# A decoder trunk on one core: four row additions placed inside VectorE's last expert round, and the closing norm worked tile by tile on three engines

## The reference

```python
logits = (x @ w_router).astype(jnp.float32) + b_router.astype(jnp.float32)
top_vals, top_idx = lax.top_k(logits, TOP_K)            # TOP_K = 2 of 8
weights = jax.nn.softmax(top_vals, axis=-1)
gates = jnp.sum(jax.nn.one_hot(top_idx, N_EXPERTS) * weights[..., None], axis=-2)
for e in range(N_EXPERTS):
    out = out + gates[..., e:e + 1] * swiglu(x, w_gate[e], w_up[e], w_down[e])
...
h = h + moe_ffn(...)
return rms_norm(h, final_norm)                          # mean of squares, rsqrt, times a gain
```

## Time and profile before

| | |
|---|---|
| time, median of 3 runs | 1004.39 us (1003.5 to 1005.32) |
| profiled execution, first to last instruction | 1002.2 us |
| PE busy | 981.9 us, 98% |
| DVE busy | 757.2 us, 76% |
| ACT busy | 656.1 us, 65% |
| POOL busy | 63.2 us, 6% |
| granted TensorE clock, mean | 0.996 of full speed |

### The profile page before, as it was taken

The page is one execution under the profiler, slowest core; times in us unless marked ns, Lnnn a source line. Parts: engine busy times, 40 slices in busy tenths (PEclk is TensorE's granted clock), DMA queues, the critical chain, the costliest instruction groups (busy, mean ns, idle before and its releaser), DMA issues.

```text
span 1002.2 us, 14574 instructions
## 1 busy us (share of the span) xinstructions
PE 981.9 (98%) x4892; PEld 830.1 (83%) x4892; DVE 757.2 (76%) x915; ACT 656.1 (65%) x886; POOL 63.2 (6%) x86
## 2 busy tenths in 40 slices
PE   8999999999999999999999999999999999999995
PEld 7988887888888899988887888888888888888883
DVE  4657665456456566766688989898998989899888
ACT  5555345453445445554697887978879787887964
POOL 1301000000000100000070000000000000000141
PEclk9999999999999999999999999999999999999998
DMA  9743589994666657243669999999999999999992
GB/s 321 231 165 126 189 249 304 289 327 154 205 203 207 210 163 201 93 136 105 221 233 398 398 383 409 390 401 378 390 375 384 406 371 400 377 382 392 381 404 108
DMA packets 150537, 287.12 MB, mean 286 GB/s; under 512 B 12770, under 2 KB 58866, under 8 KB 150499
## 3 DMA queue, kind: packets, MB, share of 16 engines
q1 hardware_dynamic: 147890, 277.64, 78.3%
q0 software_dynamic: 2608, 8.98, 2.6%
HBM read 269.81 MB, written 16.78 MB: 286 GB/s over the span
## 4 chain that ended last, share of the span: by engine, by line
PE 82%; DVE 8%; ACT 4%; DMA 3%; issue 2%; POOL 1%; SPq 0%; ACTq 0%; DVEq 0%; POOLq 0%
PE A L584 21%; PE A L586 21%; PE A L585 21%; PE S L584 4%; PE S L586 4%; PE S L585 4%; DVE lo L1608 3%; PE T L629 3%; ACT hi L1158 2%; DMA raw<-in_moe_w_down 1%; PE T L1093 1%; DMA raw<-in_moe_w_up 1%; PE T L664 1%; PE T L1051 1%; PE S L675 1%
## 5 line engine op out<-in xcount | busy, mean ns | idle before, releaser
L1608 DVE TENSOR_TENSOR lo<-raw,hi 128x1024 fp32r<-128x1024 f32 (+4 forms) x532 | 571.2, 1130 | 121.4 <-ACT hi L1158 119.4
L1158 ACT ACTIVATE hi<-raw 128x1024 fp32r<-128x1024 f32 (+4 forms) x532 | 485.5, 981 | 146.9 <-PE A L586 120.9
L584 PE MATMUL A<-lo,xT_hi 128*128 128x512 f32 x820 | 324.0, 395 | 1.7 <-DVE lo L1608 1.6
L586 PE MATMUL A<-hi,xT_hi 128*128 128x512 f32 x820 | 319.9, 390 | 0.0
L585 PE MATMUL A<-hi,xT_lo 128*128 128x512 f32 x820 | 319.6, 390 | 0.0
L584 PEld LDWEIGHTS A<-lo,xT_hi 128*128 128x128 f32 x820 | 154.2, 188 | 34.1 <-DVE lo L1608 2.4
L586 PEld LDWEIGHTS A<-hi,xT_hi 128*128 128x128 f32 x820 | 154.0, 188 | 32.4
L585 PEld LDWEIGHTS A<-hi,xT_lo 128*128 128x128 f32 x820 | 154.2, 188 | 30.3
L584 PE MATMUL S<-lo,xT_hi 128*128 128x512 f32 x224 | 89.1, 398 | 0.7 <-DVE lo L1608 0.5
L586 PE MATMUL S<-hi,xT_hi 128*128 128x512 f32 x224 | 87.5, 391 | 0.0
L585 PE MATMUL S<-hi,xT_lo 128*128 128x512 f32 x224 | 87.4, 390 | 0.0
(11 more groups left out here) (239 smaller groups left out, 871.2 us busy)
## 6 DMA issues: line engine op xcount, KB each, us to landing
raw<-in_moe_w_down SPq DMA_DIRECT2D x64, 896.0 KB, 9.2
raw<-in_moe_w_gate SPq DMA_DIRECT2D x32, 768.0 KB, 7.8
raw<-in_moe_w_up SPq DMA_DIRECT2D x24, 768.0 KB, 7.0
raw<-in_moe_w_gate SPq DMA_DIRECT2D x16, 1024.0 KB, 6.7
raw<-in_moe_w_up SPq DMA_DIRECT2D x32, 512.0 KB, 6.6
raw<-in_moe_w_up SPq DMA_DIRECT2D x16, 1024.0 KB, 7.8
raw<-in_ff_w_gate SPq DMA_DIRECT2D x10, 1024.0 KB, 8.4
raw<-in_ff_w_up SPq DMA_DIRECT2D x10, 1024.0 KB, 7.7
```

What stands on the lines that cost most here:

```text
L584: nc.tensor.matmul(out, stat[0], mov[1], start=start, stop=False)
L586: return nc.tensor.matmul(out, stat[0], mov[0], start=False, stop=stop)
L1158: return nc.scalar.activation(out, in_, ACT.Copy)
L1608: nc.vector.tensor_tensor(piece(lo, SPLIT, u, i), piece(raw, RAW, u, i), piece(hi, SPLIT, u, i).bitcast(F32), ALU.subtract).then_inc(lo_do ...
```

## The change

Five edits, all in the last round and behind it.

1. DVE's loop runs one round less (`final` = rounds - 1, computed and loaded as `nfinal`), and the body of the last round is written out behind it. In it the four `add_rows` stand behind the split of U+9: one ahead of `hidden_lo(1)`, three between it and the splits of U+10 and U+11.
2. Behind the last split come `output_lo(0)`, `output_lo(1)` and the four `add_output` in the order (0,0), (1,0), (0,1), (1,1). ACT's squares take the same order.
3. The adding of the two sums goes from POOL to DVE (`mean`); POOL is left with the power.
4. Of tile 1 DVE multiplies both halves by the gain ahead of the norm's factor; the first half then takes one multiplication on DVE (L2234 of the changed kernel), the second one on ACT as before. ACT starts the transfer of its quarter itself; SP starts three.
5. On POOL the product that gives `row_from` goes ahead, and the one that gives `gate_row` takes its place behind the wait for the stored rows.

The diff, cut to its changed lines:

```diff
@@ -329,6 +329,7 @@
         nround = sb("nround", [P, 1], I32)
+        nfinal = sb("nfinal", [P, 1], I32)
         slot_of = sb("slot_of", [P, NT, E])
@@ -388,7 +389,7 @@
         gates_set = sem("gates_set")
-        last_gained, last_out = sem("last_gained"), sem("last_out")
+        last_gained, mean_set, final_set = sem("last_gained"), sem("mean_set"), sem("final_set")
         xs_hi, xs_done = sem("xs_hi"), sem("xs_done")
@@ -432,7 +433,7 @@
 
-        gained, out_last = R2[:, 0:512], R2[:, 512:D]
+        gained, out_last = R2[:, 0:D], R2[:, D:D + 512]
         junk, junk_v, junk_end = R3[:, 3072:4096], R3[:, 2048:3072], R1[:, D:2 * D]
@@ -537,14 +538,10 @@
                     expert_loads(e, e + E)
-            for n, (t, c) in enumerate(((0, 0), (0, 1), (1, 1), (1, 0))):
+            for t, c in ((0, 0), (0, 1), (1, 0)):
                 cols = slice(c * 512, (c + 1) * 512)
-                if n == 2:
-                    sp.wait_ge(last_out, 1)
-                else:
-                    sp.wait_ge(xn_done, XN_OF["final"] + 2 * t + c + 1)
-                sp.dma_start(out[0, t * P:(t + 1) * P, cols], out_last if n == 2 else xn[:, t, cols]
-                             ).then_inc(out_done, 16)
+                sp.wait_ge(xn_done, XN_OF["final"] + 2 * t + c + 1)
+                sp.dma_start(out[0, t * P:(t + 1) * P, cols], xn[:, t, cols]).then_inc(out_done, 16)
             sp.wait_ge(out_done, 16 * 2 * NT)
@@ -1579,7 +1576,7 @@
             for n in range(4):
-                t, c = divmod(n, 2)
+                c, t = divmod(n, 2)
                 cols = slice(c * 512, (c + 1) * 512)
@@ -1588,7 +1585,9 @@
             act.wait_ge(rstd_done, N_FINAL + NT)
-            nc.scalar.activation(out_last, gained, ACT.Copy, scale=scaled(N_FINAL, 1)).then_inc(last_out, 1)
+            nc.scalar.activation(out_last, gained[:, 512:D], ACT.Copy, scale=scaled(N_FINAL, 1)).then_inc(act_step, 1)
+            act.wait_ge(act_step, 1)
+            act.dma_start(out[0, P:2 * P, 512:D], out_last).then_inc(out_done, 16)
 
@@ -2094,6 +2093,7 @@
             nc.vector.tensor_tensor(r1[:, 2, :], top[:, :, 1], top[:, :, 0], ALU.subtract).then_inc(ahead_set, 1)
+            nc.vector.tensor_scalar(nfinal[:, :], r1[:, 7, 1:2], float(E - 1), None, ALU.add).then_inc(final_set, 1)
             split(U_MOE, 0, (2,))
@@ -2159,9 +2159,11 @@
             dve.wait_ge(route_done, 1)
+            dve.wait_ge(final_set, 1)
             rounds = dve.value_load(nround[0:1, 0:1], min_val=E, max_val=2 * E)
+            final = dve.value_load(nfinal[0:1, 0:1], min_val=E - 1, max_val=2 * E - 1)
             U, t1 = U_MOE, T_MOE + 2
-            with dve.Fori(0, rounds) as ve:
+            def first_units(ve):
                 split(U + 2, ve)
@@ -2175,35 +2177,62 @@
                 split(U + 9, ve)
+
+            with dve.Fori(0, final) as ve:
+                first_units(ve)
                 hidden_lo(1, t1 + 2, ve)
...
                 split(U + 11, ve)
-                with dve.If(ve < rounds - 1):
-                    gathered_lo(t1 + 4, ve)
-                    split(U, ve + 1)
-                    split(U + 1, ve + 1)
+                gathered_lo(t1 + 4, ve)
+                split(U, ve + 1)
+                split(U + 1, ve + 1)
+
+            first_units(final)
             dve.wait_ge(gates_set, 1)
             dve.wait_ge(y_back, 16 * 2 * NT)
-            for k in range(2):
-                add_rows(k, 0)
+            add_rows(0, 0)
+            hidden_lo(1, t1 + 2, final)
+            add_rows(1, 0)
+            add_rows(0, 1)
+            add_rows(1, 1)
+            split(U + 10, final)
+            split(U + 11, final)
             output_lo(0)
-            add_rows(0, 1)
             output_lo(1)
-            add_output(0, 0)
-            add_output(0, 1)
-            add_rows(1, 1)
-            add_output(1, 0)
-            add_output(1, 1)
+            for c in range(2):
+                for t in range(NT):
+                    add_output(t, c)
             dve.wait_ge(gb2_in, 48)
+
+            def gained_last(c):
+
+                cols = slice(c * 512, (c + 1) * 512)
+                ins = nc.vector.tensor_tensor(gained[:, cols], h[:, 1, cols], GB2[:, cols], ALU.mult)
+                if c:
+                    ins.then_inc(last_gained, 1)
+                else:
+                    step(ins)
+
+            def mean(t):
+
+                dve.wait_ge(tile_summed, NT + t + 1)
+                nc.vector.tensor_scalar(rstd[:, N_FINAL, t:t + 1], half_sum[:, t, 0:1], half_sum[:, t, 1:2], EPS,
+                                        ALU.add, ALU.add).then_inc(mean_set, 1)
+
             dve.wait_ge(rows_added, 4)
-            nc.vector.tensor_tensor(gained, h[:, 1, 512:D], GB2[:, 512:D], ALU.mult).then_inc(last_gained, 1)
+            gained_last(1)
+            mean(0)
+            gained_last(0)
+            mean(1)
             dve.wait_ge(xrow_in, rounds * 16)
-            for t in range(NT):
-                dve.wait_ge(rstd_done, N_FINAL + t + 1)
-                for c in range(2 - t):
-                    cols = slice(c * 512, (c + 1) * 512)
-                    nc.vector.scalar_tensor_tensor(xn[:, t, cols], h[:, t, cols], rstd[:, N_FINAL, t:t + 1],
-                                                   GB2[:, cols], ALU.mult, ALU.mult).then_inc(xn_done, 1)
+            dve.wait_ge(rstd_done, N_FINAL + 1)
+            for c in range(2):
+                cols = slice(c * 512, (c + 1) * 512)
+                nc.vector.scalar_tensor_tensor(xn[:, 0, cols], h[:, 0, cols], rstd[:, N_FINAL, 0:1],
+                                               GB2[:, cols], ALU.mult, ALU.mult).then_inc(xn_done, 1)
+            dve.wait_ge(rstd_done, N_FINAL + 2)
+            nc.vector.tensor_scalar(xn[:, 1, 0:512], gained[:, 0:512], rstd[:, N_FINAL, 1:2], None, ALU.mult
+                                    ).then_inc(xn_done, 1)
 
@@ -2329,13 +2358,14 @@
                                             rows_n[:, t, :], None).then_inc(xg_in, 16)
+            step(nc.gpsimd.tensor_tensor(row_from[:, :, :], row_to[:, :, :], row_kept[:, :, :], ALU.mult))
             pool.wait_ge(gate_set, 1)
-            nc.gpsimd.tensor_tensor(gate_row[:, :, :], rowf[:, 1], r1[:, 5:7, :], ALU.mult).then_inc(gates_set, 1)
             pool.wait_ge(route_done, 1)
...
             pool.wait_ge(y_stored, rounds * 16 + 16)
-            step(nc.gpsimd.tensor_tensor(row_from[:, :, :], row_to[:, :, :], row_kept[:, :, :], ALU.mult))
+            nc.gpsimd.tensor_tensor(gate_row[:, :, :], rowf[:, 1], r1[:, 5:7, :], ALU.mult).then_inc(gates_set, 1)
+            pool.wait_ge(gates_set, 1)
             for k in range(2):
@@ -2343,9 +2373,7 @@
             for t in range(NT):
-                pool.wait_ge(tile_summed, 2 * t + 2)
-                step(nc.gpsimd.tensor_scalar(rstd[:, n, t:t + 1], half_sum[:, t, 0:1], half_sum[:, t, 1:2], EPS,
-                                             ALU.add, ALU.add))
+                pool.wait_ge(mean_set, t + 1)
                 nc.gpsimd.tensor_tensor(rstd[:, n, t:t + 1], rstd[:, n, t:t + 1], mhalf[:, 0:1], ALU.pow
```

## The result

The changed kernel takes **1007.99 us** (median of 5 runs, 1007.04 to 1012.85), the kernel before 1003.50 (5 runs, 1003.29 to 1005.32). The ratio is 1.0057, with an interval of 1.0044 to 1.0070: the change makes the kernel slower by about 5.7 us. The prediction was 1007.2 with 1004.8 to 1009.4. So the sign and the course of things were forecast, but the step was larger than the forecast 2.8 us: 5.7 us by the ratio and 4.5 us by the medians (two of the five runs took more than 1012 us). The time itself fell within 0.8 us of the forecast 1007.2 partly by luck, since the median of before is 0.9 us lower here than the one that the forecast started from (1003.50 against 1004.39).

A forecast was written before the change was run, and what follows sets the result against it. PE, busy for 98% of the span, was taken to bound the kernel, following DVE closely in the last round. Pause 3.7, tail -2.1 and clock +1.2 summed to +2.8 us on 1004.39, so 1007.2, range 1004.8 to 1009.4.

The forecast's parts named there:

- pause of PE: Between down(1) and down(2) of the last round, three early additions delay U+10's first piece: +3.7 us, bounds 3.5 and 3.9.
- clock: Behind PE's pause in the last round, TensorE's clock falls to 1.2 of 2.4 GHz: +1.2 us, bounds nothing and 10.
- T: Start of the last down product, 988.57 in the kernel before, forecast at 992.27 ahead of any clock cost.
- tail: From T on, the last transfer starts at T+8.8 instead of T+10.93: -2.1 us, bounds -2.8 and -1.4.
- must wait until 982.2: Behind down(1) of the last round, PE waits for U+10's first piece until 982.2: a pause of 3.9 us.
- PE has its last `down(1)` product out by 978.28: Start of PE's pause in the last round, taken as 978.05 and about 0.23 of a step.
- the clock stays up: Rival: no clock fall behind PE's pause in the last round; +1.6 us, so 1006.0; chance 0.25.
- the hold of the second power: In the tail, DVE's pair holds POOL's second power; last transfer starts at T+8.8 instead of T+8.15 with POOL undisturbed.
- stay as it is: At the span's end, the landing of the output transfers behind the last start was taken as unchanged.
- The copied round: DVE's last round written out behind the loop, new code that runs once: costed at nothing.
- Hidden, faster: Rival: rounded parts of U+10 come 3.7 us later, hiding the additions; -2.1 us, so 1002.3; chance 0.11.
- The fetched rows: Rival: rows land 3 us later, delaying the first addition; about +4.2 us, so 1008.6; chance 0.11 together with late code.

The follow-up runs named there:

- change_again: The changed kernel once more, unchanged, for a second profile and a paired ratio to the kernel before: 1009.57 us, ratio 1.0047.
- adds_alone: Kernel before with DVE's last round copied behind its loop and the four additions early as in the change, norm as before: 1009.68 us, ratio 1.0057.
- adds_behind: Changed kernel with the four row additions moved back behind the last split, the rest of the change kept: 1005.81 us, ratio 1.0015 to the kernel before.
- pause_filled: Changed kernel with 16 unused products more on PE just ahead of down(2) in the last round: 1008.56 us, ratio 1.0040 to the kernel before.
- loop_copied: Kernel before with only DVE's last round copied behind its loop and a second register load, additions and norm as before: 1004.96 us, ratio 1.0011.
- adds_behind_one_load: adds_behind with one register load on DVE ahead of the loop instead of two: 1004.52 us, ratio 1.0008 to the kernel before.
- one_early_one_load: Changed kernel with one register load, one addition ahead of hidden_lo(1) and three behind the last split: ratio 1.0009 to the kernel before.

## Why the prediction was right in direction and too small in size

The terms against the profiles, where the parts of a column sum to the difference of the spans:

| from before to the change | forecast | the change | change_again |
|---|---|---|---|
| `down(1)` ends later | 0 | 3.02 | 1.82 |
| pause of PE (first of down(2) minus last of down(1), less 0.50) | 3.7 | 5.31 | 5.33 |
| clock (first of down(2) to T) | 1.2 | 1.95 | 1.43 |
| tail | -2.1 | -1.88 | -1.88 |
| sum | 2.8 | 8.4 | 6.7 |

The timed differences, 4.5 to 5.7 us, lie below both sums. Both profiles are of long executions, and the two differ by 1.7 us, above all in the first row; how large each row is in a shorter execution isn't known.

**The pause: right mechanism, too small.** The prediction's "must wait until 982.2" rests on DVE's row of work from the first early addition (974.69) to PE's first product: 7.51 us. It measured 986.88 - 979.30 = 7.58, 985.70 - 978.11 = 7.59 and, in adds_alone, 984.33 - 976.74 = 7.59. What failed is the step "PE has its last `down(1)` product out by 978.28", 3.6 us behind DVE's first addition. That lead was taken over from before as if it were fixed. In the changed kernel it is 981.30 - 979.30 = 2.0, in change_again 980.10 - 978.11 = 2.0, in adds_alone 979.96 - 976.74 = 3.2. DVE comes late to the first addition because U+9 comes late. ACT's timeline in the changed kernel, the second half of U+9 and the first of U+10, and the latter in before:

```profile
976.30 1.79 ACT L1155 ACTIVATE hi<-raw 128x896 fp32r<-128x896 f32 x2 [1.35 <-DMA raw<-in_moe_w_down]
979.81 1.79 ACT L1155 ACTIVATE hi<-raw 128x896 fp32r<-128x896 f32 x2 [0.85 <-DMA raw<-in_moe_w_down]
```
```profile
976.42 1.79 ACT L1158 ACTIVATE hi<-raw 128x896 fp32r<-128x896 f32 x2 [2.06 <-DMA raw<-in_moe_w_down]
```

In before DVE waits twice in this place, 0.93 us for U+9 and 1.56 for U+10, and the second wait is what makes up for a late U+9. The prediction spent it on the additions (it has the idle time "hide 1.5"), and thereby also spent it as a reserve. How much of it the changed kernel had can be estimated. In before DVE's split starts 0.98 us behind ACT's rounding of the same piece (976.42 to 977.40), so here it could have started at 979.81 + 0.98 = 980.79; without additions `hidden_lo(1)` would have ended at 979.30 + 1.15 = 980.45. That leaves 0.34 us to hide in and not 1.5. In change_again the same sum gives 0.34, in adds_alone 0.80. The split starts at 985.74, 4.95 us later than it could have; the other 0.4 us of the pause in the table would have come without any addition.

adds_alone bears it out in part: with a lead of 3.2 its pause, counted as the forecast counts, is 984.33 - 979.96 = 4.4, against 3.9. Why the weights of the last round land later in the changed kernel than in adds_behind, whose instructions up to this place are the same, stays open.

**The clock: right in kind, somewhat too small.** It fell in the pause (3.6 us in, in change_again 2.5), stood at 0.50, and cost 1.95, 1.43 and, in adds_alone, 11.34 - 10.02 = 1.3 us, where 1.2 was forecast. The forecast took it that PE works 2.2 us at the lower level; it was 4.8, 3.7 and 3.4 us. pause_filled takes it away and nothing else. The rival "the clock stays up" has fallen. The Trainium skill (TensorE: Matmul & The Clock Gate, section "HAM oscillation — how this bites in real kernels") tells of bursts that start slow behind a pause for data; the traces agree: 8 to 11 slow products, most at a step of 0.43 us, behind pauses of 4.2 to 5.4.

**The tail: the sum right, its parts not.** SP's last transfer starts at 1007.1, T+8.25, sooner than the T+8.8 for which the powers were to be held; one takes 0.95 us, the other 0.54, and DVE's pair starts 0.12 us behind the start of the latter. So the hold of the second power, for which the sum had 0.65 us (T+8.8 against T+8.15), didn't come. In return the landing doesn't "stay as it is": four transfers start within a microsecond (1006.1 to 1007.1) and the longest lands 3.0 us after its start, against 2.3 at most before. By adds_behind and adds_alone the whole gain is that of the moved additions; the new order of the norm costs 0.2 to 0.3 us in the profiles (11.75 against 11.53, 13.88 against 13.55 in loop_copied). That the sum came out within 0.2 us is in part luck.

**The copied round: costed at nothing, costs 1.1 us** (loop_copied, 1.0003 to 1.0020). Neither the second load nor the sooner scatter is shown to be the reason. With adds_behind_one_load the weights come late too, with one_early_one_load they don't, though DVE's instructions up to the last round are the same. Where the lateness arises is known, the first expert round; why stays open.

**The other rivals.** "Hidden, faster" has fallen, and not because the rounded parts of U+10 came in time: they came 3.4 us later than in before (980.79 by the estimate, against 977.40), near the 3.7 of the rival. But all that stands ahead of them came later still, so there was nothing to hide in. The rival held U+10 late with U+9 in its old place. The fetched rows were never waited for at the first addition: DVE has no idle time ahead of it in any profile.

## What to carry to other kernels

Work moved ahead of the bottleneck's end must fit into the gap that is idle there, and a gap behind late data is a reserve, too: what is put into it costs on the day when the data come later. Here one addition of 1.28 us fitted in two profiles, the fourth part of what was moved; all four stopped PE for 5.4 us to save 1.9. Even the one is close: in adds_behind and loop_copied, where nothing stands in the gap, it is only 1.04 and 1.11 us long. Price a pause of TensorE at more than its length (1.3 to 1.95 us beyond it here), and don't pay for a shorter tail with work on the path of the busiest engine.

## What the runs showed of the hardware

- The granted clock fell 3.6 us behind the start of the pause in the changed kernel, 2.5 in change_again and 4.8 in adds_alone, in the last case when products ran again. It was back 6.8, 6.8 and 3.4 us later, so the same event costs differently from one run to the next. The stretches of change_again:

```profile
982.50:983.00 0.50, 0.00 (x0) 0.00 (x0) 0.50 (x1) 0.05 (x2) 0.00 (x0) 0.57 0.28 115
989.00:989.50 0.50, 0.50 (x3) 0.40 (x2) 0.50 (x1) 0.00 (x0) 0.00 (x0) 0.60 0.00 0
```

and of adds_alone:

```profile
988.00:988.50 0.50, 0.50 (x3) 0.40 (x2) 0.50 (x2) 0.00 (x0) 0.00 (x0) 0.84 0.00 0
```

- A POOL product of 128x4 took 0.29 us where it came ahead of a row of DVE's splits and 2.34 us where it met it, and so 0.6 us more idle time on DVE (1.76 against 1.15, which a second register load gives) let POOL's scatter start 1.7 us sooner. The Trainium skill (SBUF — State Buffer, section "SBUF: two separate sides") has the two engines lock each other out of a shared port; the trace agrees, and adds the size.
- Four output transfers that start within 1 us land up to 3.0 us after their start, against 2.1 to 2.3 when they are spread over 2.6 us. The same 3.0 stands in one_early_one_load.
